# The second block's first norms as one stage, with the z and narrow projections of each tile between the turns of the next

## What is computed

```
x = first_block(...)                       # ends in a norm with final_g
hx = rms_norm(x, norm1) * (1 + sc1) + sh1
hc = rms_norm(ctx, norm1) * (1 + csc1) + csh1
zx, xbc_x, dt_x, qx, kx, vx = split_projection(hx @ w_in)
zc, xbc_c, dt_c, qc, kc, vc = split_projection(hc @ w_in)
```

## Time and profile before

| | |
|---|---|
| median of 3 runs | 4900.81 us (4894.11 to 4903.95) |
| the profiled execution | 4908.46 us, of which the span of the trace is 4906.8 us |
| PE busy | 4213.9 us (86%) |
| DVE busy | 1584.1 us (32%) |
| ACT busy | 774.9 us (16%) |
| POOL busy | 407.3 us (8%) |
| norm stages n3 and n4 | 2820.3 to 2929.9 us |
| stage proj | 2929.9 to 3268.2 us |

### The profile page before, as it was taken

One profiled execution on the slowest core, in us unless ns is written; L12 is line 12 of the kernel. 1 busy time (PEld: TensorE's weight loads), 2 busy tenths in 40 slices (PEclk: granted clock), 3 DMA queues, 4 the chain that ended last, 5 costly groups with the idle time before them and its releaser, 6 DMA issues. The chain is left out here.

```text
span 4906.8 us, 43985 instructions
## 1 busy us (share of the span) xinstructions
PE 4213.9 (86%) x15266; PEld 2372.8 (48%) x15266; DVE 1584.1 (32%) x3374; ACT 774.9 (16%) x1759; POOL 407.3 (8%) x386
## 2 busy tenths in 40 slices
PE   5799999987869999999999819987988499999851
PEld 3466666665424444444444314456764444444320
DVE  4577777773350000000000053329433100000004
ACT  2233333331100000000000011111541010010000
POOL 0111111110000000000000000015000100000001
PEclk8899999998869999999999959988899599999875
DMA  6211111102379898888888531100112289999744
GB/s 254 51 36 38 38 38 34 38 22 111 144 280 339 305 312 310 306 309 311 303 308 313 187 141 28 26 5 1 66 57 101 52 320 336 332 335 336 266 156 173
DMA packets 440267, 872.94 MB, mean 178 GB/s; under 512 B 95345, under 2 KB 139201, under 8 KB 433977
## 3 DMA queue, kind: packets, MB, share of 16 engines
q1 hardware_dynamic: 412201, 779.00, 45.5%
q0 software_dynamic: 20800, 73.57, 4.5%
q10 hardware_dynamic: 7120, 18.49, 1.0%
HBM read 798.54 MB, written 72.47 MB: 178 GB/s over the span
## 5 line engine op out<-in xcount | busy, mean ns | idle before, releaser
L1814 PE MATMUL moe_gbank<-moe_ring,moe_xT 128*128 128x512 f32 x1536 | 679.5, 595 | 3.9 <-ACTq L1870 3.9
L1832 PE MATMUL moe_acc<-moe_ring,moe_hidT 128*128 128x512 f32 x1536 | 675.1, 592 | 1.8 <-DVEq L1929 1.1
L1814 PE MATMUL moe_ubank<-moe_ring,moe_xT 128*128 128x512 f32 x1536 | 675.1, 592 | 0.0
L1904 DVE TENSOR_TENSOR moe_hid<-moe_sg,moe_ubank 128x512 f32<-128x512 f32 x96 | 66.0, 688 | 1658.4 <-PE moe_ubank L1814 1658.4
L921 PE MATMUL gdn_pbank<-mix_xT,gdn_w 128*128 128x512 f32 (+1 forms) x1280 | 542.0, 557 | 2.2 <-PEq L815 2.2
L1814 PEld LDWEIGHTS moe_gbank<-moe_ring,moe_xT 128*128 128x128 f32 x1536 | 293.3, 191 | 373.5 <-issue 370.3
L1832 PEld LDWEIGHTS moe_acc<-moe_ring,moe_hidT 128*128 128x128 f32 x1536 | 288.2, 190 | 347.1 <-issue 347.1
L1814 PEld LDWEIGHTS moe_ubank<-moe_ring,moe_xT 128*128 128x128 f32 x1536 | 284.5, 190 | 322.4 <-issue 322.4
L921 PEld LDWEIGHTS gdn_pbank<-mix_xT,gdn_w 128*128 128x128 f32 x1280 | 229.4, 194 | 162.4 <-issue 154.4
L1875 ACT ACTIVATE moe_sg<-moe_gbank 128x512 f32<-128x512 f32 x96 | 57.3, 597 | 1547.2 <-PE moe_gbank L1814 1547.2
L2050 PE MATMUL proj_abank<-mix_yT,proj_wq 128*128 128x512 f32 x416 | 180.8, 592 | 0.6 <-PE proj_abank L2050 0.6
(11 more groups left out here) (510 smaller groups left out, 5057.5 us busy)
## 6 DMA issues: line engine op xcount, KB each, us to landing
moe_ring<-in_moe_w_gate SPq DMA_DIRECT2D x64, 2048.0 KB, 7.8
moe_ring<-in_moe_w_up SPq DMA_DIRECT2D x64, 2048.0 KB, 8.6
moe_ring<-in_moe_w_down SPq DMA_DIRECT2D x64, 2048.0 KB, 7.7
moe_ring<-in_w_gate SPq DMA_DIRECT2D x32, 2048.0 KB, 9.2
moe_ring<-in_w_up SPq DMA_DIRECT2D x32, 2048.0 KB, 9.8
moe_ring<-in_w_down SPq DMA_DIRECT2D x32, 2048.0 KB, 10.6
front_wt<-in_w_mod SPq DMA_DIRECT2D x24, 1024.0 KB, 13.7
route_wt<-in_w_ada SPq DMA_DIRECT2D x24, 1024.0 KB, 14.7
```

The lines of the kernel that those rows point to most:

```text
L1814: last = nc.tensor.matmul(bank[:], xT[:, k, :], w[:, k * 512:(k + 1) * 512], start=(k == 0), stop=(k == KD - 1))
L1832: last = nc.tensor.matmul(acc[j][:], hidT[:, k, :], w[:, k * D + j * 512:k * D + (j + 1) * 512], start=(f == 0 and k == 0), stop=(f == NF ...
L1904: nc.vector.tensor_tensor(hid[:], sg[:], ubank[:], ALU.mult).then_inc(u_free, 1)
```

## The change

n3 and n4 become one stage, `norms_and_narrow` (name n34), over all 10 tiles. Of each tile DVE now does only the two multiplications, the shift and the inverse roots; ACT makes the squares with their sum and the root. There are 4 buffers of x. The loop of z and the narrow columns leaves `project`: PE does it in n34, `narrow(t - 1)` after `turn(t)`. z is copied unchanged there, and one SiLU over all of it (128 x 4096) stands at the end of ACT's program in `project`. All loads of n34 are on SP's queue, in this order: 2 context tiles; gain, context scale and shift; 2 latent tiles; `final_g`, latent scale and shift; `wv` in two parts; `wz`; the other 6 latent tiles as buffers come free; then the convolution's weights `cwr` and the first two `wq` of `project`, whose arrival the stage waits for. Buffers that nothing else uses yet (BC, xs, qT) hold the shifts, scales, gains, squares and `wz`.

```diff
-def norm_mod_transpose(nc, name, tiles, shift_scale, gain, ident, xT=None, rows_out=None, first_norm=None):
...
+def norms_and_narrow(nc, ctx_rows, x_rows, x1_rows, shift_scale, gain, g_first, w_in, conv_w, conv_b, ident, xT, BC, xs, qT, z, dtr, vtok, cwr, wq):
+    NB, NY = 4, 3
+    XT = 8
+    n = NC_T + NT
+    W2 = 2 * SH + KVH * HD
+    with Stage(nc, "n34") as st:
+        x = [st.sb(f"x{i}", [P, D]) for i in range(NB)]
+        y = [st.sb(f"y{i}", [P, D]) for i in range(NY)]
+        wv = st.sb("wv", [P, KD, W2])
+        ss, root, mean = (st.sb(s, [P, 2 * n]) for s in ("ss", "root", "mean"))
+        step, eps = st.sb("step", [P, 1]), st.sb("eps", [P, 1])
+        sh, sc = [BC[:, i, 0:D] for i in (0, 1)], [BC[:, i, 0:D] for i in (2, 3)]
+        gb, g0, sq = qT[:, 0, :], qT[:, 1, :], qT[:, 2, :]
+        wz = xs[:, 0:KD, :]
+        tp = [[st.ps(f"tp{i}_{j}", [P, 512]) for j in range(2)] for i in range(2)]
+        zbank = [st.ps(f"zbank{i}", [P, 512]) for i in range(2)]
+        vbank = [st.ps(f"vbank{i}", [P, 512]) for i in range(2)]
...
+        def load_tile(w, dst_, i):
+            for half in range(2):
+                c = XBC0 + i * P
+                w.dma_start(dst_[:, 4 * half:4 * half + 4, :], w_in[4 * half * P:4 * (half + 1) * P, c:c + P].rearrange("(k p) n -> p k n", p=P)).then_inc(next_loaded, 16)
+        with nc.Block() as block:
+            @block.sync
+            def _(sp):
+                def load_x(t):
+                    sp.dma_start(x[t % NB][:], ctx_rows[t] if t < NC_T else x_rows[t - NC_T]).then_inc(x_loaded[t % NB], 16)
+                for t in range(NC_T):
+                    load_x(t)
+                sp.dma_start(gb, row_view(gain)).then_inc(par_loaded, 16)
+                for i in (1, 0):
+                    sp.dma_start(sc[i], row_view(shift_scale[i][1])).then_inc(par_loaded, 16)
+                    sp.dma_start(sh[i], row_view(shift_scale[i][0])).then_inc(par_loaded, 16)
+                    if i:
+                        for t in range(NC_T, NB):
+                            load_x(t)
+                        sp.dma_start(g0, row_view(g_first)).then_inc(par_loaded, 16)
+                with nc.allow_non_contiguous_dma("narrow blocks"):
+                    sp.dma_start(wv[:, :, 0:2 * SH], w_in[:, DT0:Q0].rearrange("(k p) n -> p k n", p=P)).then_inc(w_loaded, 16)
+                    sp.dma_start(wv[:, :, 2 * SH:], w_in[:, V0:INC].rearrange("(k p) n -> p k n", p=P)).then_inc(w_loaded, 16)
+                sp.dma_start(wz, w_in[:, 0:SI].rearrange("(k p) n -> p k n", p=P)).then_inc(w_loaded, 16)
+                for t in range(NB, n):
+                    sp.wait_ge(y_ready, t - NB + 1)
+                    if t - NB >= NC_T:
+                        sp.wait_ge(kept[t % NB], 16 * len(range(NC_T + (t - NC_T) % NB, t - NB + 1, NB)))
+                    load_x(t)
+                sp.dma_start(cwr[0:CONV * XT, :], conv_w.rearrange("j (a p) -> (j a) p", p=P)).then_inc(next_loaded, 16)
+                sp.dma_start(cwr[CONV * XT:, :], conv_b.rearrange("(a p) -> a p", p=P)).then_inc(next_loaded, 16)
+                with nc.allow_non_contiguous_dma("columns of one head"):
+                    for i in range(2):
+                        load_tile(sp, wq[i], i)
+                sp.wait_ge(next_loaded, 96)
+            @block.tensor
+            def _(pe):
+                def turn(t):
+                    pe.wait_ge(y_ready, t + 1)
+                    if t >= 2:
+                        pe.wait_ge(t_out, t - 1)
+                    for k in range(KD):
+                        last = nc.tensor.transpose(tp[t % 2][k // 4][:, (k % 4) * P:(k % 4 + 1) * P], y[t % NY][:, k * P:(k + 1) * P], ident)
+                    last.then_inc(t_ready, 1)
+                def narrow(t):
+                    pe.wait_ge(t_out, t + 1)
+                    src, c = (xT[0], t * P) if t < NC_T else (xT[1], (t - NC_T) * P)
+                    if t >= NC_T:
+                        q = t - NC_T
+                        if q >= 2:
+                            pe.wait_ge(z_out, q - 1)
+                        for k in range(KD):
+                            last = nc.tensor.matmul(zbank[q % 2][:], src[:, k, c:c + P], wz[:, k, :], start=(k == 0), stop=(k == KD - 1))
+                        last.then_inc(z_full, 1)
+                    if t >= 2:
+                        pe.wait_ge(v_out, t - 1)
+                    for k in range(KD):
+                        last = nc.tensor.matmul(vbank[t % 2][:, 0:W2], src[:, k, c:c + P], wv[:, k, :], start=(k == 0), stop=(k == KD - 1))
+                    last.then_inc(v_full, 1)
+                turn(0)
+                pe.wait_ge(w_loaded, 48)
+                for t in range(1, n):
+                    turn(t)
+                    narrow(t - 1)
+                narrow(n - 1)
+            @block.scalar
+            def _(act):
+                done = 0
+                def squares(t, norm):
+                    nonlocal done
+                    if t < NC_T or norm == 0:
+                        act.wait_ge(x_loaded[t % NB], 16 * (t // NB + 1))
+                    else:
+                        act.wait_ge(first_ready, t - NC_T + 1)
+                        act.dma_start(x1_rows[t - NC_T], x[t % NB][:]).then_inc(kept[t % NB], 16)
+                    q = 2 * t + norm
+                    nc.scalar.activation(sq, x[t % NB][:], ACT.Square, accum_out=ss[:, q:q + 1]).then_inc(sq_ready, 1)
+                    done += 1
+                    act.wait_ge(sq_ready, done)
+                    nc.scalar.activation(root[:, q:q + 1], ss[:, q:q + 1], ACT.Sqrt, bias=eps[:], scale=1.0 / D).then_inc(root_ready, 1)
+                def turned_out(t):
+                    act.wait_ge(t_ready, t + 1)
+                    dst, c = (xT[0], t * P) if t < NC_T else (xT[1], (t - NC_T) * P)
+                    for j in range(2):
+                        last = nc.scalar.activation(dst[:, 4 * j:4 * j + 4, c:c + P], tp[t % 2][j][:].rearrange("p (k n) -> p k n", k=4), ACT.Copy)
+                    last.then_inc(t_out, 1)
+                def z_rows(t):
+                    if t >= NC_T:
+                        q = t - NC_T
+                        act.wait_ge(z_full, q + 1)
+                        nc.scalar.activation(z[:, q, :], zbank[q % 2][:], ACT.Copy).then_inc(z_out, 1)
+                act.wait_ge(eps_ready, 1)
+                for t in range(NC_T):
+                    squares(t, 1)
+                for t in range(NC_T, NC_T + 2):
+                    squares(t, 0)
+                for t in range(NC_T, n):
+                    squares(t, 1)
+                    if t + 2 < n:
+                        squares(t + 2, 0)
+                    turned_out(t - 2)
+                    if t >= 3:
+                        z_rows(t - 3)
+                turned_out(n - 2)
+                z_rows(n - 3)
+                turned_out(n - 1)
+                z_rows(n - 2)
+                z_rows(n - 1)
+                for i in range(NB):
+                    act.wait_ge(kept[i], 16 * len(range(NC_T + (i - NC_T) % NB, n, NB)))
+            @block.vector
+            def _(dve):
+                def rstd(t, norm, at):
+                    q = 2 * t + norm
+                    dve.wait_ge(root_ready, at)
+                    nc.vector.tensor_scalar(mean[:, q:q + 1], ss[:, q:q + 1], 1.0 / D, EPS, ALU.mult, ALU.add)
+                    refined_rsqrt(dve, nc.vector, root[:, q:q + 1], mean[:, q:q + 1], step[:])
+                    dve.drain()
+                    return root[:, q:q + 1]
+                def first(t):
+                    s1 = rstd(t, 0, first_at[t])
+                    nc.vector.scalar_tensor_tensor(out=x[t % NB][:], in0=x[t % NB][:], scalar=s1, in1=g0, op0=ALU.mult, op1=ALU.mult).then_inc(first_ready, 1)
+                def second(t):
+                    s1 = rstd(t, 1, second_at[t])
+                    pair = 1 if t < NC_T else 0
+                    if t >= NY:
+                        dve.wait_ge(t_ready, t - NY + 1)
+                    nc.vector.scalar_tensor_tensor(out=y[t % NY][:], in0=x[t % NB][:], scalar=s1, in1=sc[pair], op0=ALU.mult, op1=ALU.mult)
+                    dve.drain()
+                    nc.vector.tensor_tensor(y[t % NY][:], y[t % NY][:], sh[pair], ALU.add).then_inc(y_ready, 1)
+                def narrow_rows(t):
+                    dve.wait_ge(v_full, t + 1)
+                    nc.vector.tensor_copy(dtr[:, t, :], vbank[t % 2][:, 0:2 * SH])
+                    nc.vector.tensor_copy(vtok[:, t, :], vbank[t % 2][:, 2 * SH:W2])
+                    dve.drain()
+                    dve.sem_inc(v_out, 1)
+                nc.vector.memset(eps[:], EPS).then_inc(eps_ready, 1)
+                dve.wait_ge(par_loaded, 96)
+                for i in (1, 0):
+                    nc.vector.scalar_tensor_tensor(out=sc[i], in0=sc[i], scalar=1.0, in1=gb, op0=ALU.add, op1=ALU.mult)
+                dve.drain()
+                for t in range(NC_T):
+                    second(t)
```

(63 more changed lines are left out.)

129 lines of the change are left out of this document (19 added, 110 removed).

## The result

| | before | after |
|---|---|---|
| median of 4 runs | 4897.60 us | 4826.52 us |
| lowest to highest | 4894.11 to 4903.95 | 4822.32 to 4827.62 |
| ratio after/before, 95% interval | | 0.9847 (0.9836 to 0.9859) |
| profiled execution | 4908.46, span 4906.8 | 4826.77, span 4825.1 |

The change makes the kernel 1.5% faster. (One more execution of the kernel before joined the three from above, so its median is not quite 4900.81; its profile is the one shown.) The prediction of 4829 is 2.5 us above the median. What its sum is about can be read in place, since every step of it has a row after the change.

What follows compares the result with a forecast made beforehand. DVE was taken to bound n4 and PE the last part of proj, in sequence. +0.2 us ahead of proj's first main matmul and -72.3 behind it made -72.1, from 4900.81 to 4829 us; range 4815 to 4850.

Steps and rivals of the forecast that it cites:

- What was removed behind the first main matmul: End of proj: without the loop, DVE's rotation of k follows at once, at 3190.75 instead of 3263.06; -72.3 us.
- (1): Start of the new stage: DVE waits for all six parameter rows, 17 us after the first load, range 14 to 20.
- (2): DVE's first norms in the new stage: y of tile 0 at 23.0 us, of tile 1 at 26.5.
- (3): New stage's start: copies PE wants queue behind ACT's later squares; first narrow product at 33.2 us, stream from 42.1.
- (4): Stream of latent tiles: PE is the bound at 9.70 us a tile, DVE 6.4; 75.9 us in all.
- 1.5 us set aside for a rising clock: Stream of latent tiles: 1.5 us added for a clock that rises only during the first tile.
- Rival B: PE stays at half clock through the stream: 75.9 us more, 4905 us, no change; chance 0.03.
- (5): From stream's end to proj's first main matmul: copies 0.5 and stage change 2.3 us, reaching it at 122.3.
- The weights: wv and wz, behind the parameters in SP's queue: there at 25.8 us, first needed at 33.2, slack 7.4.
- Rival A: New stage: a late supply or handoff holds PE up some 2 us a tile or 15 once; 4845 us, chance 0.12.
- C: New stage: engines hand one tile round without overlapping, PE cold at each; 24.0 us a tile, 4945 us, chance 0.02.
- D: End of proj: something else ends it late, only the SiLU could, by 4.3 us at most; no separate chance.

Runs made afterwards that it cites:

- experiments on the start: Four versions of the kernel after, with split load waits and then changed orders of loads, ACT and DVE: 4819.18, 4821.82, 4825.56 and 4815.21 us.
- the norms alone: Kernel after, but with z and the narrow columns left in a loop at the end of proj: 4853.88 us, ratio to before 0.9894.
- experiment 4: Kernel after, but with the convolution's weights and first two wq loaded in proj again, behind the stage change: 4835.48 us, ratio to before 0.9858.
- experiment 3: Kernel after, but with the squares and their sums back on DVE: 4840.99 us, ratio to before 0.9867.
- experiment 6: Kernel after with DVE's and PE's load waits split: 4819.18 us; then also wz behind one more x load and ACT's first copies earlier: 4821.82 us.

## Why the prediction was right, step by step

**What was removed behind the first main matmul.** Forecast -72.3, measured -72.4. The reading of the earlier trace rows held: what is won is DVE's free time from 3190.75 to 3263.06, not PE's 74.6 us of loop. The SiLU took 3.62 us, where 4.3 had been scaled from the one of 1282 elements; it was hidden as argued.

**(1) and (2), the parameters and DVE's start.** 17 forecast, 17.3 measured, and 16.6, 16.4 and 17.1 in the other executions. The y of the second tile was forecast for 26.5, and the turn that it releases begins at 2850.53 - 2823.51 = 27.0. Taking the four loads of n4 with those in flight beside them as the base, and not the rate of the earlier trace rows by itself (13.3), was the right choice.

**(3), ACT's order.** The first narrow product at 33.4 (forecast 33.2), ended by ACT's copies as named, at half clock: 2860.70 - 2856.89 = 3.8 (3.9). The stream from 42.5 (42.1). This was the step without a row of its own, and was built up from the squares of out2. The experiments on the start show that the wait it named is real and not all: taking it away uncovers a late x load, then a late y, then the copies of the next tile.

**(4), the stream.** Forecast 9.70 us a tile with PE as the bound; measured 9.70 in the kernel after and with DVE's squares back, and 6.27 with half of z. From the first z to the end of the last narrow product it is 2939.89 + 1.96 - 2865.98 = 75.9, as forecast. The 1.5 us set aside for a rising clock were not needed: the window 2860 to 2865 is at 0.95 already. This is the one term of the sum that was clearly mis-sized; with 0.4 us more at the start and 0.1 more on the way out it makes the 1.0 us between 122.3 and 121.3. DVE took some 9.70 - 3.41 = 6.3 us a tile (forecast 6.4) and waited for PE the other 3 (3.06, 3.41).

Rival B was half clock through the stream. The stream is at 1.00 and never waits. What the rival was about is seen where PE does wait: with 1.35 us of idle time ahead of the first z or of the turn before it (kernel after) z took 6.87 us, with 3.14 us 7.47 (and the turn before it some 0.8 more), with 4.33 us 9.63 and with 5.42 us 9.88. The Trainium skill, "TensorE: Matmul & The Clock Gate", section "HAM oscillation", describes just this, a burst of matmuls that starts slow behind each wait. Its mechanism is seen at the stream's start in three experiments. In the norms alone PE waits 3.74 us a tile and the clock is 0.50 throughout, so there it never rises to fall back. The trace of the kernel after shows that products laid end to end are out of its reach.

**(5), the way out.** 2.9 us from the end of the last narrow product to the first main matmul (2944.77 - 2941.85), forecast 0.5 + 2.3. The first sixteen main matmuls took 5.41 us in this execution, about as in the kernel before, and 3.72 in the other three: the 1.8 us that the prediction had in its low bound came there. The preload was worth 8 to 10 us, as experiment 4 shows.

**The weights.** `wv` and `wz` had arrived when PE first wanted them: the bracket before the first narrow product names ACT's copies, not a load. `wz` landed some 11.6 us after its issue at 2836.57, 24.7 after the first load (forecast 25.8). The rule of the Trainium skill, "DMA: Bandwidth & Descriptors", that line rate needs pieces of 512 B, changed nothing in the sum: the part with smaller pieces was in time, and no run here measured its rate alone.

**Rival A**, a late supply, is not what happened in the kernel after, but it is what bounded the experiments on the start: with DVE's wait split, a load (3.55 us) and ACT's order (8.24 us) were next. **Rivals C and D** did not happen.

**What the number alone could not tell.** The range reached to 4850 and so held rival A's 4845; it is the turns 9.70 us apart and the start at 42.5 that part the two, not the median. One sentence of the prediction does not hold as it stands: that DVE's relief from 8.52 to 6.4 us a tile helps to pay for PE's 9.70. In the stream it pays nothing (experiment 3: the same 9.70 with the squares back on DVE). What is measured of the pay for PE's work is some 13 us by the squares on ACT, all ahead of the stream, and some 6 by the preloads up to the first main matmul. What pays the rest of the 44.0 us that z and the narrow columns cost there was not taken apart.

**Between sum and measurement.** The sum said -72.1, the rows say -73.3, and the medians of the four comparisons -71.1, -77.9, -73.3 and -86.2, each of which carries the spread of its runs. That 4829 came within 2.5 us of the first median is therefore partly luck; that the rows came within 1.2 us of the sum is not. The two profiles differ by 81.7, and whoever took this number would credit the change with 8 us that are mostly attention's clock.

## What to carry to other kernels

Where a stage bound by DVE is followed by one bound by PE on the same data, laying one under the other costs only the larger of the two a tile; work out each engine's time a tile, and take as the gain where the loop leaves the idle time of the engine that waits last (here DVE's 72.3 us), not the length of the loop. Set against it what the stage that takes the loop in gets longer (here 44.0): the move alone was worth some 29. Once the stream runs, relief for an engine under the bound is worth nothing; what is left is its start, where each engine's fixed order decides. There, put what feeds the bounding engine ahead of work for later tiles, and follow each wait taken away to the next: the three versions in which another wait came in ahead of the first z gained 1 to 6 us, and the one in which none did 9.6.

## What the runs showed of the hardware that I had not expected

- **A load can hold its queue.** The second part of `wv` took 6.63 us to issue on SP's queue, and `wz` behind it 3.65 (the other loads before them 0.4 to 1.0; the same part of `wv` took 5.83 to 7.04 in every other run that has it there). Issued after a pause, `wz` took 0.44. In the kernel before the same part of `wv` had taken 0.93 on POOL's queue. That a full queue is the cause is not shown. What is issued behind goes out late, by about 1 us for the x load of experiment 6; most of ACT's 3.55 us there is the load's own 10.0 us on the way.
- **A wait of 3 to 5 us costs the matmuls behind it 0.6 to 3.0 us** (7.47, 9.63 and 9.88 against 6.87 for the same sixteen), one of 1.35 us nothing. Each of the three longer waits was seen once.
- **Attention has two lengths**, 192.5 to 193.4 and 200.9 to 201.4 us, in executions of the same kernel, with a granted clock of 0.93 or 0.76 over 50 us in which PE is about equally busy (0.73 in the kernel before). What decides between them stays open.
